# Three-block transformer kernel on one core: where the last weight units of a stage are split, which PSUM banks a group uses, how x, the result and the parameters are laid out, and the order of the embedding gates

## What is computed

```python
for i in range(2):
    x = x + 0.5 * rmsnorm(swiglu(rmsnorm(x, g), w_gate, w_up, w_down), g2)  # d_ff 2816
    h = rmsnorm(x, g)          # w_in; stick-breaking + latent attention, short conv; w_out
    x = x + rmsnorm(mixed @ w_out, g)
    x = x + 0.5 * rmsnorm(swiglu(...), g)
    x = x + rmsnorm(sigmoid(rmsnorm(x, g) @ w_ple_gate) * (p @ w_ple_proj), g)
# second_block
x = x + rms_norm((gate_pool * y_pool + gate_rnn * y_rnn) @ w_o, g)       # pooling, RG-LRU
x = x + rms_norm((gelu(conv(h @ w_gate)) * (h @ w_up)) @ w_down, g)      # d_ff 3072
x = x + sigmoid(rms_norm(x, g) @ w_ple_gate) * rms_norm(p @ w_ple_proj, g)
```

## Time and profile before

| what | value |
|---|---|
| median of three runs | 3087.11 us |
| the profiled execution, its own time | 3083.58 us |
| its span in the trace | 3081.8 us |
| PE busy | 2957.9 us, 96% of the span |
| DVE, ACT busy | 1591.5 us (52%), 1169.7 us (38%) |
| mean granted TensorE clock | 0.981 |
| matmuls | 14,474 |

### The profile page before, as it was taken

One profiled execution on the slowest core, in us unless ns is written; L12 is line 12 of the kernel. 1 busy time (PEld: TensorE's weight loads), 2 busy tenths in 40 slices (PEclk: granted clock), 3 DMA queues, 4 the chain that ended last, 5 costly groups with the idle time before them and its releaser, 6 DMA issues.

```text
span 3081.8 us, 36164 instructions
## 1 busy us (share of the span) xinstructions
PE 2957.9 (96%) x14474; PEld 2454.3 (80%) x14474; DVE 1591.5 (52%) x2407; ACT 1169.7 (38%) x1901; POOL 38.6 (1%) x47
## 2 busy tenths in 40 slices
PE   8999999999999989999999999999889999999998
PEld 7788887578888878888876588888777778888887
DVE  5543256646442464442546564442675646666337
ACT  4332243544232453332525353222643435332234
POOL 0000000000000000000000000000000100000000
PEclk9999999899999989999999999999999999999999
DMA  4233313022333223333232023333222222332331
GB/s 136 89 97 99 107 58 90 25 62 83 96 97 99 79 69 103 96 96 96 83 79 60 24 87 96 96 96 103 76 72 87 85 82 83 103 101 91 103 103 55
DMA packets 201192, 264.96 MB, mean 86 GB/s; under 512 B 34903, under 2 KB 154177, under 8 KB 201025
## 3 DMA queue, kind: packets, MB, share of 16 engines
q1 hardware_dynamic: 200464, 262.46, 27.9%
q10 hardware_dynamic: 561, 0.19, 0.0%
HBM read 258.41 MB, written 2.10 MB: 85 GB/s over the span
## 4 chain that ended last, share of the span: by engine, by line
PE 79%; DVE 9%; ACT 5%; DMA 3%; issue 2%; ACTq 0%; SPq 0%; DVEq 0%
PE ps L502 24%; PE ps L504 24%; PE ps L503 24%; DVE WL L417 2%; ACT WH L412 2%; PE ps L904 2%; DMA raw<-in_w_in 1%; DMA raw<-in_w_up 1%; PE ps L911 1%; DVE HL L1444 1%; PE ps L890 1%; DVE X L1553 1%; DVE Y L1547 1%; DVE U L1533 1%; ACT HH L1053 1%
## 5 line engine op out<-in xcount | busy, mean ns | idle before, releaser
L502 PE MATMUL ps<-HH,WH 128*128 128x512 f32 (+1 forms) x3200 | 1170.1, 366 | 49.0 <-DVE WL L417 37.9
L417 DVE TENSOR_TENSOR WL<-raw,WH 128x1024 fp32r<-128x1024 f32 (+1 forms) x490 | 590.9, 1209 | 1172.3 <-ACT WH L412 1171.7
L503 PE MATMUL ps<-HH,WL 128*128 128x512 f32 (+1 forms) x3200 | 1156.7, 361 | 0.0
L504 PE MATMUL ps<-HL,WH 128*128 128x512 f32 (+1 forms) x3200 | 1156.5, 361 | 0.0
L412 ACT ACTIVATE WH<-raw 128x1024 fp32r<-128x1024 f32 (+1 forms) x490 | 510.0, 1044 | 1204.5 <-PE ps L504 1068.1
L502 PEld LDWEIGHTS ps<-HH,WH 128*128 128x128 f32 x3200 | 610.6, 191 | 149.0 <-DVE WL L417 43.9
L503 PEld LDWEIGHTS ps<-HH,WL 128*128 128x128 f32 x3200 | 610.9, 191 | 92.7 <-issue 1.9
L504 PEld LDWEIGHTS ps<-HL,WH 128*128 128x128 f32 x3200 | 610.5, 191 | 90.3
L502 PE MATMUL ps<-HIDH,WH 128*128 128x512 f32 (+1 forms) x1056 | 381.6, 361 | 13.3 <-ACT Y L1046 13.3
L503 PE MATMUL ps<-HIDH,WL 128*128 128x512 f32 (+1 forms) x1056 | 379.9, 360 | 0.0
L504 PE MATMUL ps<-HIDL,WH 128*128 128x512 f32 (+1 forms) x1056 | 379.7, 360 | 0.0
(11 more groups left out here) (246 smaller groups left out, 2155.3 us busy)
## 6 DMA issues: line engine op xcount, KB each, us to landing
raw<-in_w_up SPq DMA_DIRECT2D x272, 256.0 KB, 3.1
raw<-in_w_down SPq DMA_DIRECT2D x112, 512.0 KB, 3.5
raw<-in_w_gate SPq DMA_DIRECT2D x176, 256.0 KB, 2.8
raw<-in_w_in SPq DMA_DIRECT2D x68, 512.0 KB, 3.6
raw<-in_w_ple_gate SPq DMA_DIRECT2D x24, 512.0 KB, 3.7
raw<-in_w_out SPq DMA_DIRECT2D x16, 512.0 KB, 3.7
raw<-in_w_rg_out SPq DMA_DIRECT2D x8, 512.0 KB, 3.5
raw<-in_w_o SPq DMA_DIRECT2D x8, 512.0 KB, 3.6
```

Source lines behind the costliest of these rows:

```text
L417: e.tensor_tensor(WL[tile_of[u]][:, 0:n], raw[u % NRAW][:, 0:n], WH[tile_of[u]][:, 0:n].bitcast(F32), ALU.subtract).then_inc(*low.done((u,)))
L502: e.matmul(o, wh, ah, start=start, stop=False, skip_group_check=skip)
L503: e.matmul(o, wl, ah, start=False, stop=False, skip_group_check=skip)
L504: return e.matmul(o, wh, al, start=False, stop=stop, skip_group_check=skip)
```

## The change

The units of a stage that are passed in halves at its end (the four held units) get the split tiles WH4 to WH7 instead of the next stage's first four, which go round the ring (`held`, `tiles`, `tiles_free`). Groups of an FFN, and the first two of the layers' mixers, alternate between banks 0 to 3 and 4 to 7. x and the result are laid out by columns on the host, p too, and the parameters come as one array of 128x362; the transposes and copies for them go. The first eight units have raw buffers of their own. The second squares matmul moves from i 1 to i 3. The rotary tables move into the down projection, behind its unit 10. In the embeddings stage all four held units are split ahead of the scale R, only two of the next stage's first units ahead of the gates of columns 4 to 7, the third and fourth between them, and the last gate's product and square are moved ahead.

```diff
-        own = {u: NSPLIT + i for s in range(1, len(STAGES)) for i, u in enumerate(self.first(s))}
+    def held(self, s):
+
+        kind = STAGES[s]
+        if s == LAST:
+            return [self[s, "proj", c] for c in range(2)] + [self[s, "gate", 1, kp] for kp in range(2)]
+        if kind == "ple":
+            return [self[s, "gate", 1, kp] for kp in range(4)]
+        name, count = {"ffn": ("down", (FF2 if s > 8 else FF) // P), "mix": ("out", 8), "mix2": ("o", 8)}[kind]
+        return [self[s, name, k] for k in range(count - 4, count)]
...
+        own = {u: NSPLIT + i for s in range(len(STAGES)) for i, u in enumerate(self.held(s))}
...
-            if s and STAGES[s - 1] == "ffn":
-                e.wait_ge(*pe.at("unit", W[s - 1, "down", (11, 5, 9, 13)[tile_of[u] - NSPLIT]]))
+            if s is not None and STAGES[s] == "ffn":
+                e.wait_ge(*pe.at("unit", W[s, "down", (11, 5, 9, 13)[tile_of[u] - NSPLIT]]))
...
+        raw += [hid_tile(f"first_raw{i}", [P, UNIT], 28 + 4 * i) for i in range(FIRST)]
...
-            for t in range(2):
-                e.dma_start(xtok[:, t, :], a["x"][0, t * P:(t + 1) * P, :]).then_inc(*x_in[t // 2].done(("x", t)))
+            e.dma_start(X[:, :, part(0)], a["x"][0]).then_inc(*x_in[0].done(("x", 0)))
...
-                if u >= NRAW:
+                if u >= FIRST + NRAW:
...
-            e.wait_ge(*stored.at("out", 1, TC - 1))
+            for n in range(DC):
+                e.wait_ge(*vec.at("x_out", n))
+                e.dma_start(out[n], X[:, n, :]).then_inc(*stored.done(("out", n)))
...
-                        if s and h == 0 and kp == 1 and i == 1:
+                        if s and h == 0 and kp == 1 and i == 3:
                             tensor_second_squares(e, s - 1, 4)
...
+        def group_banks(g):
+
+            return range(4) if g % 2 == 0 else range(4, DC)
+
+        def second_free(s):
+
+            if STAGES[s] == "ple":
+                return [[act.at("y_scale", s, 1)], [vec.at("gated", s, 1, 5)], [vec.at("gated", s, 1, 6)]]
+            return [[act.at("y_scale", s, 1)], [y_at(s, 1, 5)], [y_at(s, 1, 6)]]
...
-                tensor_group(e, s, f"gate_up{g}", [W[s, "gu", g, kp] for kp in range(4)], cols, range(4),
-                             [[vec.at("evacuated", s, g - 1, i)] for i in range(4)])
+                if g > 1:
+                    free = [[vec.at("evacuated", s, g - 2, i)] for i in range(4)]
+                else:
+                    free = second_free(s - 1) + [[act.at("x_scale", s)]] if s else [[], [], [], [act.at("x_scale", s)]]
+                tensor_group(e, s, f"gate_up{g}", [W[s, "gu", g, kp] for kp in range(4)], cols, group_banks(g), free)
...
-                if c == 0 and i == 1 and s < LAST:
+                if c == 0 and i == 3 and s < LAST:
                     tensor_second_squares(e, s - 1, 7)
...
-            in_group(1, with_rope, range(4), [[vec.at("in", s, 0, b)] for b in range(4)])
-            in_group(2, wide, range(4), [[vec.at("in", s, 1, b)] for b in range(4)], {1: turn_values})
-            in_group(3, narrow, range(2), [[vec.at("in", s, 2, b)] for b in range(2)])
-            in_group(4, wide, range(4), [[vec.at("in", s, 3 if b < 2 else 2, b)] for b in range(4)])
+            in_group(1, with_rope, range(4, DC), second_free(s - 1) + [[act.at("x_scale", s)]])
+            in_group(2, wide, range(4), [[vec.at("in", s, 0, b)] for b in range(4)], {1: turn_values})
+            in_group(3, narrow, (5, 7), [[vec.at("v_turned", s, 1)], [act.at("latent_scale", s, 0)]])
+            in_group(4, wide, range(4), [[vec.at("in", s, 2, b)] for b in range(4)])
...
-                if g == 1 and s == 0:
-                    vector_tables(e)
             for k in range(4, 2 * n_groups):
                 split_low(e, W[s, "down", k])
+                if s == 0 and k == 10:
+                    vector_tables(e)
...
+            for u in held_units[s]:
+                split_high(e, u)
             scalar_x_scale(e, s)
-            split_high(e, rest[1])
             for n in range(4):
                 scalar_sigmoid(e, s, n, slice(0, T), ("gate", s, n))
-            split_high(e, rest[2])
-            split_high(e, rest[3])
...
+            split_low(e, units[2])
             gate(1, 4)
             gated(1, 4)
             for m in range(3):
                 vector_update(e, s, 0, m)
                 if m:
                     gated(1, 4 + m)
+                if m == 2:
+                    split_low(e, units[3])
                 gate(1, 5 + m)
                 vector_y_sum(e, s, 1, 4 + m)
-            gated(1, 7)
-            vector_update(e, s, 0, 3)
+            vector_update(e, s, 0, 3, lambda: gated(1, 7))
```

278 lines of the change are left out of this document (109 added, 169 removed).

## The result

The changed kernel takes 2993.4 us (median of 4 runs, 2991.3 to 2997.5), against 3087.8 before (median of 4, 3087.0 to 3089.5): a ratio of 0.9695, 95% interval 0.9678 to 0.9712, 94.4 us less. It was forecast at 3001, in a range of 2987 to 3030. The profiled execution is the slowest of the four, 2997.5 us, and that of the kernel before was 4.2 us faster than its median, so the traces show 86 of the 94 us.

What follows compares the result with a forecast made beforehand. PE's stream of matmuls was taken to bound the kernel. Terms summing to 89.4 us, less 3.0 for seams, took 3083.6 to 2997.2; 3.5 to the median gave 3001 us, range 2987 to 3030.

Steps and rivals of the forecast that it cites:

- The start: At the kernel's start, PE begins earlier without parameter loading and copies of x: 11.5 us gained (8 to 13.5).
- The rotary tables: At 95.03 us, PE's stop while DVE makes the tables, and the slow clock after it, go: 4.0 us.
- The held units: At stage ends, PE's eight stops on ACT's copy of an output tile go, with slow clock behind five: 28.7 us.
- The banks: At group changes in FFN stages and mixers, PE's stops on DVE's evacuation of bank 0 go: 18.3 us.
- the token transposes: Eight token transposes, costing 1.03 us in each of three stages, go: 3.0 us.
- The squares: At six seams, PE's 0.80 us wait for DVE's sum goes, as other matmuls come first: 4.8 us.
- The embeddings stages: In both embeddings stages, new ACT and DVE order brings the gates earlier: 8.0 and 7.3, together 15.3 us (0 to 19).
- The allowance at the seams: PE reaches ten seams earlier than DVE's chain was laid out for: 0.3 us off each, 3.0 in all.
- that the stops at the groups are waits for units: Rival: group stops are waits for split units, so other banks don't help; 18.3 us stay, 3019 us; chance 0.12.
- that the embeddings stages gain nothing: Rival: R, behind four splits, delays the gates as much as later splits did; 15.3 us stay, 3016; chance 0.12.
- that the stop moves to group 1 of each stage: Rival: next stage's units come late in the ring, costing 3.2 us at ten seams, 3033 us; chance 0.08.
- The slower pace of the matmuls: Rival: all through the program matmuls slow down; from 2.7% no gain, 4% would give 3126 us; chance 0.02.

Runs made afterwards that it cites:

- experiment 9: Kernel four_more with unit 0 sent ahead of x, x's first half in two pieces, and ACT and DVE reordered in the embeddings stages: 2962.9 us (0.9609).
- experiment 2: Changed kernel with all groups of the five FFN stages on banks 0 to 3 again, mixers keeping their other banks: 3012.0 us (0.977).
- experiment 5: Changed kernel with the matmul of the second half's sum of squares put back from column block 3 to column block 1: 2998.1 us (0.9721).
- experiment 6: Changed kernel with the sum of squares of x's second half in bank 6 in place of 7: span 2987.0 us, one execution.
- experiment 4: Changed kernel with ACT's and DVE's earlier order in the two embeddings stages, held units still in tiles of their own: 3004.5 us (0.9744).
- experiment 1: Changed kernel with the extra tiles given back to the next stage's first four units at five of the ten seams: 3011.3 us (0.9768).
- experiment 3: Changed kernel with the edits of experiment 1 and experiment 2 at once: 3027.7 us (0.9816).
- four_more: Changed kernel plus experiment 6's edit, other banks in the third block's mixer, and a split and scale moved ahead in the embeddings stages: 2973.6 us (0.9639).
- no_first_raw: Changed kernel without the eight raw buffers for the first units, which go through the two ordinary ones: span 2989.1 us, one execution.

## Why the prediction was right, point by point

The forecast was 7.6 us above the median. The terms, in the order of the sum:

- **The start** (11.5): group 1 starts at 37.45 in place of 48.91, 11.5 earlier. The first split was forecast at 8.3 and is at 8.45, PE's first matmul at 11.2 and is at 11.31; what remains of the stop at unit 2 is 0.20, not 1.2, since PE's first matmuls started 0.21 us apart, the pace of the lower clock, and used up the difference. The fit of the Trainium skill (DMA: Bandwidth & Descriptors, Anatomy of one DMA — SWDGE (gpsimd) path), 2.0 us plus the bytes over 436 GB/s, had given 6.4 for x and unit 0. The page gives that fit for DMAs issued from GpSimd, and these go out on SP's queue. In the trace x's first half is there at 6.83 and unit 0 at 8.34. In experiment 9 unit 0 is the first thing sent, in two DMAs at 0.74 and 1.24, and it is there at 5.11, 4.4 after the first, where the fit gives 3.2 for its 512 KB, so that taking the trace's rows was right. Once it runs, the queue moves about 350 GB/s: between 17.86 and 25.36 ten DMAs of 256 KB land. The same page (Where 436 GB/s comes from) has about 358 as the HBM limit of a core, and the trace agrees with that figure.
- **The rotary tables** (4.0): no stop from 23 to 398 and no slow clock from 14 on. The first landmark comes 19.9 us earlier; start, tables and the stop of the held units there (2.44 + 1.69) add up to 19.6.
- **The held units** (28.7): half of it was tested. Five seams were expected to be worth 14.4 and measured 13.7 by the spans and 17.9 by the medians. The other three have no stop in the trace; they weren't undone. The step was right: the wait on the copy came back at each seam where the tiles were swapped back, with a slow clock behind three of the five.
- **The banks** (18.3) **and the token transposes** (3.0): the stops that they name have no row in the trace of after. But as a price of the banks they are undersized. For the FFN stages the two terms hold 10.1 + 2.1 = 12.2, with the 1.0 at the first group change that stands under the start; undone, the banks alone cost 18.6 to 19.4, of which 16.7 are stops and the clock behind them. The step that failed is reading the worth of an edit from the stop as it stands. The stop had 1.03 us of transposes in front of it in two stages, and had no slow clock behind it there (1.94 and 1.88 us before), where the longer ones of experiment 2 have 1.7 each. For the change as a whole this did no harm, because it removes stop and cover at once. The banks of the mixers, 9.2 of the 18.3, and the transposes were not undone.
- **The squares** (4.8): wrong, 0.0 at the seams. It did bring 1.4 us behind each of the two embeddings stages (experiment 5), which the prediction counted in their term. The sentence that failed is that the six stops of 0.80 go and nothing is late next. What is late next is R, which ACT and DVE finish at their own pace, and PE waits for it 16 us further on, 0.74 us in place of 0.80. The prediction looked for a new wait at group 1 and at the input's low part, and not at the other matmul on a sum of squares, which waits for ACT because it shares bank 7. Experiment 6 took that wait away and got 1.0 us at a seam.
- **The embeddings stages** (15.3): undone, their order cost 13.2 by the landmarks, 11.1 by the medians and 8.4 by the profiled spans, in which less slow clock in attention hides the rest. The stop on the last sum is 6.00; some 5 was forecast. Measured from the first sum of squares of the stage before, it ends 6.0 us earlier than in the kernel before (83.8 against 89.8), and 6.1 in the second such stage; 6.6 was forecast.
- **The end** (3.8): DVE's last update of x ends 2.4 us before the span does, against 6.3 before, so 3.9.
- **The allowance at the seams** (3.0): 5.4 us of waits on R, at six seams, 0.9 each, where the prediction allowed 0.3 at each of ten. With the 4.8 that the squares didn't bring it is one and the same error.
- **The third block's mixer**: not in the sum, and some 5 us slower in this execution. From the second sum of squares of stage 7 to the first of stage 8 the changed kernel gains only 0.2 us, although the stop of the held units with its slow clock (2.03 + 1.71) lies there and went. The first stop is 2.30 us and not 1.01, and three stops are followed by a slow clock, 5.1 us in all, where one was before, 1.7. In the second profile of the changed kernel it is two, and 1.01.
- What made up for it is no term either: the attention parts lost 16.7 us to slow clock in the profile of before and 13.6 in this one.

The rivals: that the stops at the groups are waits for units fell with experiment 2; that the embeddings stages gain nothing, with experiment 4; that the stop moves to group 1 of each stage, with the trace, which has no such stop outside the third block's mixer. The slower pace of the matmuls didn't show, 226 ns in both kernels (4% would have given 3127, not 3126).

What made the time come out lower than forecast by 7.6 us isn't a term of the sum. The profiled execution, at 2997.5, meets the sum's 2997.2. But the forecast put the median 3.5 us above the profile, as before, and here it is 4.1 below: the other three runs are 3 to 6 us faster, and the traces of two such executions of this kernel show that most of the difference is slow clock.

That the sum meets the profiled execution to 0.3 us is in part luck. Without the allowance the terms add up to 89.4, and the trace has 86.1. Between the landmarks most terms are right to within 0.8 us. But the two layers' mixers gained 2.2 us more each than their terms, 1.5 of it slow clock in attention, the third block's mixer 4.7 less, and the last stretch 1.7 less, which is the wait on R. The allowance of 3.0 stands about where these cancel, and was taken off for another reason. In all, experiments 1, 2 and 4 gave back 17.9, 18.6 and 11.1 of the 94.4 us. The start but for its buffers, the tables, three of the eight held seams, the banks of the mixers, the transposes and the end are read from the trace alone.

## What to carry to other kernels

When an edit removes a stop, ask which chain the waiting engine will meet next, and follow that chain back to whether it hangs on the moved work at all: two engines in step with each other set the end of a seam, and the third only chooses where it waits. A stop that the profile puts down to one operand is often the queue of the engine named, and splitting by bank or by tile what stands behind that queue is worth more than the stop, since the clock that follows it and the work that hid part of it count too. Buffers that nobody waits for, like the eight at the start, cost memory and brought nothing in the one execution that tested it.

## What the runs showed of the hardware

The clock is a term of its own, and the length of a stop doesn't tell whether it falls. A fall in the middle of PE's work cost 1.7 us, 3.4 or 5.1; where PE stopped meanwhile, it cost less of its work, 1.4 to 2.7 around the stops of 6.0 us. Before, stops of 2.76 (at 424.95), 2.75 and 2.32 us had none behind them, and one of 2.03 had. At one and the same stop, 2.51 us ahead of the second product of the third block's mixer, no clock was lost before, and 1.65 us with the change; nor was any in experiments 1, 3, 5 and 6, which have the same stop. At the one in the middle of that mixer, 3.48 and 3.36 us long in the two profiles of the changed kernel, 1.7 were lost in one and 3.0 in the other. What can be said is that fewer stops went with less loss, but loosely: 44.4 us before with 124 us of idle PE, 22.6 and 19.9 in the two profiles of the changed kernel with 75 and 73; four_more, with 57 us idle, lost 12.8, but six_more, with 50, lost 17.8, and no_first_raw, with the stops of the changed kernel, only 16.5.

The attention parts lose clock in every profile, on stops of 0.5 to 1.3 us that come close together, but not the same amount: between the landmarks of stages 4 and 5 the two profiles of the changed kernel differ by 3.3 us with the same program and the same stops. This is most of the 3.7 us, 0.1%, between the two, and a term of a few us can't be judged by a median here.

Two sums of squares in one bank, for two halves of the tokens, tie PE to ACT although they touch different columns, because the kernel waits before it writes into a bank that ACT still reads. The Trainium skill (PSUM — Partial Sum Buffer, PSUM bank collisions raise a hardware error) has the reason: two engines must not use one bank at once, and the hardware reports an error instead of making one wait. No run here tried that; all of them wait. Giving the second one a bank of its own, which was free at that point, was worth some 7 us over the program (experiment 6, one execution).
